# Two transformer blocks on one core: pool sums ahead of the rotary tiles, rotary partners shuffled on VectorE, and the FFN root applied to the up products

## What is computed

```python
def first_block(x, ...):
    h = rmsnorm(x, attn_norm[l])
    z = h @ w_in[l]                     # pool input, q, k, v, gates
    a = pool_mixer(u_pool, w_pool[l], pool_scale[l])     # windows 2, 4, 8, 16
    q = partial_rope(rmsnorm(q, q_norm[l]), positions) * scale
    k = partial_rope(rmsnorm(k, k_norm[l]), positions)
    b = swa_sink_attention(q, k, v, sinks[l])
    x = x + (g_pool * a + g_attn * b) @ w_out[l]
    h = rmsnorm(x, ffn_norm[l])
    up = causal_depthwise_conv(h @ w_up[l], conv_w[l], conv_b[l])
    gate, val = up[..., :D_FF], up[..., D_FF:]
    x = x + (jax.nn.silu(gate) * val) @ w_down[l]
...
def partial_rope(x, positions):         # first 16 of each head's 64 channels
    x1, x2, xp = xf[..., :half], xf[..., half:ROPE_DIM], xf[..., ROPE_DIM:]
    out = jnp.concatenate([x1 * cos - x2 * sin, x2 * cos + x1 * sin, xp], axis=-1)
...
def rmsnorm(x, g):
    r = lax.rsqrt(jnp.mean(xf * xf, axis=-1, keepdims=True) + EPS)
    return (xf * r * g.astype(jnp.float32)).astype(x.dtype)
```

## Time and profile before

| | us |
|---|---|
| median of 3 runs | 1557.7 (1555.8 to 1557.96) |
| the profiled execution: its time | 1557.63 |
| its span, first to last instruction | 1555.4 |
| PE busy in the span | 1422.1 (91%) |
| POOL busy | 782.1 (50%) |
| DVE busy | 666.7 (43%) |
| ACT busy | 420.2 (27%) |

### The profile page before, as it was taken

One profiled execution on the slowest core, in us unless ns is written; L12 is line 12 of the kernel. 1 busy time (PEld: TensorE's weight loads), 2 busy tenths in 40 slices (PEclk: granted clock), 3 DMA queues, 4 the chain that ended last, 5 costly groups with the idle time before them and its releaser, 6 DMA issues.

```text
span 1555.4 us, 20333 instructions
## 1 busy us (share of the span) xinstructions
PE 1422.1 (91%) x7602; PEld 1160.6 (75%) x7602; DVE 666.7 (43%) x1016; ACT 420.2 (27%) x833; POOL 782.1 (50%) x459
## 2 busy tenths in 40 slices
PE   5898789987999999999897999985997999999996
PEld 3776567766888888888796888755985888888884
DVE  5139455654534344211434888468625111211112
ACT  3132234431221112110323445452433111111111
POOL 4554234335566666666071633222362766666661
PEclk9999889998999999999998999996999999999998
DMA  4221121112232222222120111100020323322221
GB/s 171 82 81 68 35 74 55 67 40 97 76 100 95 94 94 94 96 98 90 43 96 27 41 58 53 56 0 2 2 78 31 121 95 99 101 97 94 94 81 54
DMA packets 31883, 114.00 MB, mean 73 GB/s; under 512 B 3536, under 2 KB 4048, under 8 KB 31568
## 3 DMA queue, kind: packets, MB, share of 16 engines
q1 hardware_dynamic: 31824, 113.16, 21.9%
HBM read 111.05 MB, written 2.10 MB: 73 GB/s over the span
## 4 chain that ended last, share of the span: by engine, by line
PE 81%; DVE 12%; ACT 3%; issue 2%; DMA 1%; POOL 0%; SPq 0%; DVEq 0%; ACTq 0%; POOLq 0%
PE ps L995 40%; PE ps L1189 17%; PE ps L1336 5%; ACT arena L542 3%; PE ps L1014 2%; PE ps L1035 2%; PE ps L1028 2%; PE ps L1209 1%; DVE arena L1948 1%; PE ps L1310 1%; PE ps L1140 1%; DVE arena L1613 1%; PE ps L1129 1%; DVE h_lo L1599 1%; DVE arena L1661 1%
## 5 line engine op out<-in xcount | busy, mean ns | idle before, releaser
L461 POOL TENSOR_SCALAR w_hi<-raw 128x1024 fp32r<-128x1024 f32 x204 | 220.0, 1078 | 650.8 <-PE ps L995 219.0
L463 POOL TENSOR_TENSOR w_lo<-raw,w_hi 128x1024 fp32r<-128x1024 f32 x204 | 512.2, 2511 | 17.1
L995 PE MATMUL ps<-h_hi,w_hi 128*128 128x512 f32 (+1 forms) x976 | 378.7, 394 | 12.9 <-ACT arena L542 7.4
L995 PE MATMUL ps<-h_lo,w_hi 128*128 128x512 f32 (+1 forms) x976 | 371.4, 386 | 0.0
L995 PE MATMUL ps<-h_hi,w_lo 128*128 128x512 f32 (+1 forms) x976 | 371.3, 386 | 0.0
L995 PEld LDWEIGHTS ps<-h_hi,w_hi 128*128 128x128 f32 x976 | 184.3, 191 | 58.7 <-issue 14.6
L995 PEld LDWEIGHTS ps<-h_lo,w_hi 128*128 128x128 f32 x976 | 184.0, 191 | 37.8 <-issue 2.5
L995 PEld LDWEIGHTS ps<-h_hi,w_lo 128*128 128x128 f32 x976 | 183.5, 190 | 36.5
L542 ACT ACTIVATE arena<-ps 128x512 f32<-128x512 f32 (+7 forms) x213 | 101.0, 509 | 308.0 <-PE ps L995 103.6
L542 ACT ACTIVATE arena<-arena 128x512 f32<-128x512 f32 (+6 forms) x190 | 101.0, 534 | 217.5 <-DVE arena L2193 134.2
L1189 PE MATMUL ps<-g_hi,w_hi 128*128 128x512 f32 x400 | 155.6, 389 | 0.0
(11 more groups left out here) (266 smaller groups left out, 1824.1 us busy)
## 6 DMA issues: line engine op xcount, KB each, us to landing
raw<-in_w_stream SPq DMA_DIRECT2D x204, 512.0 KB, 3.5
xT<-in_x_t SPq DMA_DIRECT2D x2, 1056.0 KB, 6.7
out<-xT SPq DMA_DIRECT2D x8, 256.0 KB, 2.1
C<-in_cst SPq DMA_DIRECT2D x1, 640.0 KB, 9.6
arena<-in_cst SPq DMA_DIRECT2D x1, 528.0 KB, 3.4
arena<-in_pos SPq DMA_DIRECT2D x1, 256.0 KB, 3.9
V<-in_vec SPq DMA_DIRECT2D x1, 174.5 KB, 8.1
band<-in_cst SPq DMA_DIRECT2D x1, 160.5 KB, 3.5
```

Source lines behind the costliest of these rows:

```text
L461: pool.tensor_scalar(w_hi[j][:], raw[j % 2][:], 1.0, 1.0, ALU.mult, ALU.mult).then_inc(S["pool_step"], 1)
L463: pool.tensor_tensor(w_lo[j][:], raw[j % 2][:], w_hi[j][:], ALU.subtract).then_inc(split_done[j], 1)
L995: last = mm(dst[p], w[:, k, :], h[:, k, cols], start=(k == 0 and n == 0), stop=(k == KT - 1 and n == 2))
```

## The change

Three parts.

1. **First rotary stage and pool sums.** `rot1` and the products by it go. DVE instead moves the partners with a `stream_shuffle` inside groups of 32 partitions (`ROT1`), and the sign goes into the sine table. `qk(t)` now starts when `qgb` is there and waits for the root only ahead of its last multiplication; `qk_side` no longer waits for `qk_dve`. On DVE all four `windows` and the first two `window_parts` stand ahead of `qk(0)`.
2. **Second rotary stage.** The same with `ROT2`: the products by `rot2` go, and two waits of `k2_side` with them.
3. **FFN.** The up products are made of x times gain without the root. ACT writes `h_hi` as x times gain as soon as the last `w_out` product is done, DVE subtracts (`low_of`); `sum_all(1)` stands behind the first pair of up tiles. DVE multiplies every one of the 44 up tiles by the root, in PSUM, before ACT reads it (`up_scaled`), and does so one tile ahead of the taps.

```diff
@@ -317,7 +304,7 @@
-            "up_act dve_up up_read silu_ready m1_ready relu_ready m2_ready ms_hi ms_ready f2_ready "
+            "up_scaled up_act dve_up up_read silu_ready m1_ready relu_ready m2_ready ms_hi ms_ready f2_ready "
@@ -397,6 +388,9 @@
+        ROT1 = [(m + 8 if m < 8 else m - 8) if m < 16 else m for m in range(32)]
+        ROT2 = [(m + 16) % 32 for m in range(32)]
...
@@ -667,11 +660,16 @@
-            for f in range(KT):
+            for f in range(KT - 1):
                 act.wait_ge(S["x_ready"], f + 1)
                 square(1, f, xT[:, f, REAL], T)
+            product(act, U_OUT + 7)
+            for f in range(KT):
+                if f == 2:
+                    act.wait_ge(S["x_ready"], KT)
+                    square(1, KT - 1, xT[:, KT - 1, REAL], T)
+                a(h_hi5[:, f, :], xT[:, f, REAL], ACT.Copy, scale=vcol("ffn_norm", f)).then_inc(S["hi_ready"], 1)
             root(1, ps[:, 7, :], first)
-            high(2, REAL)
...
@@ -1052,15 +1050,12 @@
             def qk_side(t):
                 pe.wait_ge(S["tile_read"], (9 if t == 0 else t + 10))
                 wait(pe, S["qk_sqrt"], t - 1)
-                wait(pe, S["qk_dve"], t - 1)
-                mm(ps[:, 2 + t % 2, :], cst_ap("blk64"), sqb[:, t % 2, :], start=True, stop=True)
-                mm(ps[:, 4 + t % 2, :], rot1, qgb[:, t % 2, :], start=True, stop=True).then_inc(S["qk_side"], 1)
+                mm(ps[:, 2 + t % 2, :], cst_ap("blk64"), sqb[:, t % 2, :], start=True, stop=True).then_inc(S["qk_side"], 1)
@@ -1159,13 +1154,12 @@
-            sum_all(1)
-
             def up(i):
                 for q in range(4):
                     if isinstance(i, int) and q < 2:
                         if q == 0:
                             tile_pair(U_UP, 2, [[ps[:, 0, :]], [ps[:, 1, :]]])
+                            sum_all(1)
                         continue
@@ -1235,14 +1229,10 @@
                 wait(pe, S["k2_sqrt"], t)
-                wait(pe, S["k2_dve"], t)
...
-                for c in range(2):
-                    last = mm(ps[:, 6 + c, 0:HALF], cst_ap("rot2"), val2[t % 2][:, halves[c]], start=True, stop=True)
@@ -1681,34 +1671,28 @@
             def qk(t):
                 out_ = KA if t == 0 else Q[:, t - 1, :]
-                dve.wait_ge(S["qk_sqrt"], t + 1)
+                dve.wait_ge(S["tile_read"], (9 if t == 0 else t + 10))
...
+                step(v.stream_shuffle(t2, qgb[:, t % 2, :], ROT1))
                 step(v.tensor_tensor(t1, qgb[:, t % 2, :], rope_c, ALU.mult))
-                step(v.tensor_tensor(t2, ps[:, 4 + t % 2, :], rope_s, ALU.mult))
+                step.settle()
+                step(v.tensor_tensor(t2, t2, rope_s, ALU.mult))
                 step.settle()
                 step(v.tensor_tensor(t1, t1, t2, ALU.add))
                 step.settle()
+                dve.wait_ge(S["qk_sqrt"], t + 1)
                 v.tensor_tensor(out_, t1, rs[:, t % 2, :], ALU.mult).then_inc(S["qk_dve"], 1)
...
+            for g in range(4):
+                windows(g)
+                if g < 2:
+                    window_parts(g)
+            for t in range(9):
+                qk(t)
             window_parts(2)
             window_parts(3)
...
+            def low_of(name, n, f):
+                dve.wait_ge(S["hi_ready"], parts_before(n) + f + 1)
+                v.scalar_tensor_tensor(out=h_lo5[:, f, :], in0=xT[:, f, REAL], scalar=vcol(name, f), in1=h_hi5[:, f, :],
+                                       op0=ALU.mult, op1=ALU.subtract).then_inc(S["h_ready"], 1)
...
-            add_squares(1, 7)
+            for f in range(KT):
+                low_of("ffn_norm", 2, f)
+                if f == 2:
+                    add_squares(1, 7)
             dve.wait_ge(S["rs_ready"], 2)
-            parts(2, REAL, gained("ffn_norm", REAL))
@@ -1815,6 +1806,12 @@
+                        if h == 0 and e == 0:
+                            product(dve, U_UP, i)
+                            v.tensor_tensor(ps[:, 0, :], ps[:, 0, :], n_ri[:, 0:T], ALU.mult).then_inc(S["up_scaled"], 1)
+                        if q < 3:
+                            product(dve, U_UP + q + 1, i)
+                            v.tensor_tensor(ps[:, q + 1, :], ps[:, q + 1, :], n_ri[:, 0:T], ALU.mult).then_inc(S["up_scaled"], 1)
                         dve.wait_ge(S["up_act"], 4 * i + q + 1)
```

More of the change, by code:

```diff
@@ L65 @@
     NV += _w
-_C = [("ident", P), ("blk64", P), ("rot2", P), ("swap", P), ("upto_f", P), ("upto_b", P),
+_C = [("ident", P), ("blk64", P), ("swap", P), ("upto_f", P), ("upto_b", P),
       ("past_f", P), ("past_b", P), ("neg_f", P), ("neg_b", P)]
@@ L74 @@
     NCST += _w
-NC1 = P + 256 + 64 + 1
+NC1 = 256 + 64 + 1
 NC2 = 2 * L
@@ L90, in constants @@
     put("swap", (i[:, None] == (i[None, :] + 64) % P).astype(np.float32))
-    rot2 = np.zeros((P, P), np.float32)
-    for m in range(P):
-        if m % 32 < 16:
-            rot2[m + 16, m] = -1.0
-        else:
-            rot2[m - 16, m] = 1.0
-    put("rot2", rot2)
     put("upto_f", (i[:, None] <= i[None, :]).astype(np.float32))
@@ L104, in constants @@
     c1 = np.zeros((P, NC1), np.float32)
-    for m in range(P):
-        if m % 64 < 8:
-            c1[m + 8, m] = -1.0
-        elif m % 64 < 16:
-            c1[m - 8, m] = 1.0
     k = np.arange(256)
     ok = (k[None, :] <= i[:, None] + P) & (i[:, None] + P - k[None, :] < P)
-    c1[:, P:P + 256] = np.where(ok, 0.0, -1e30)
+    c1[:, 0:256] = np.where(ok, 0.0, -1e30)
     for g, w in enumerate((2, 4, 8, 16)):
-        c1[:, P + 256 + 16 * g:P + 272 + 16 * g] = np.minimum(np.arange(16) + 1, w)
+        c1[:, 256 + 16 * g:272 + 16 * g] = np.minimum(np.arange(16) + 1, w)
     inv = np.float32(500000.0) ** (-np.arange(0, 16, 2, dtype=np.float32) / np.float32(16))
-    c1[:, NC1 - 1] = np.where(i % 64 < 16, inv[i % 8], 0.0)
+    c1[:, NC1 - 1] = np.where(i % 64 < 8, -inv[i % 8], np.where(i % 64 < 16, inv[i % 8], 0.0))
     t = np.arange(T)
@@ L681, in up @@
                         q = 2 * h + e
-                        product(act, U_UP + q, i)
+                        act.wait_ge(S["up_scaled"], 4 * i + q + 1)
                         if isinstance(i, int):
```

42 lines of the change are left out of this document (13 added, 29 removed).

## The result

The changed kernel takes 1539.2 us (median of 4 runs, 1536.5 to 1542.7) where the kernel before takes 1557.0 in the same session (4 runs, 1555.8 to 1558.0). The ratio is 0.9887 with a 95% interval of 0.9866 to 0.9909: 17.8 us faster. The forecast was 1536.3 with a range of 1526 to 1543.

The account below looks back on a forecast made before the run. The prediction took TensorE to bound the kernel (81% of the span, VectorE 12%). Gains of 12.7, 4.9 and 3.7 sum to 21.3 us: span 1534.1, time 1536.3, range 1526 to 1543.

Parts of the forecast that it names:

- Part 1: First rotary stage and pool sums: `pooled(0)` starts at 157.5 against 170.25, 12.7 us sooner.
- the period: First rotary stage, from query tile 2 on: a tile and one side product, 6.32 us, with DVE keeping up.
- the last step: End of the first rotary stage: `qk(7)`'s last multiplication at +4.7, then five instructions, `pooled(0)` 8.2 us behind query tile 8.
- Part 2: Second rotary stage: four side products fewer on the path, 3.55, and 2.1 at the end, less 0.7: 4.9 us faster.
- the later start of wide tile 2: Second rotary stage: DVE's shuffle and multiplications take turns with POOL's split, so wide tile 2 starts 0.7 us later (0 to 1.4).
- Part 3: FFN: 4.8 us gained at the third up tile, 1.1 waited at the down products: 3.7 us faster.
- The fourth: FFN: the pair of up tiles keeps its 12.46 us, clock included, since TensorE is still idle 4.6 us ahead of it.
- what follows is unchanged: Behind each mark on TensorE's list: later stages take the same time, so gains are not taken back.
- A: First rotary stage: pool sums hidden, no wait at the swap, part 1 gives 21 us, time 1528; chance 17%.
- B: First rotary stage: turns cost more, key tile 3 us later or periods add 4 to 6, time 1540 to 1543; 16%.
- C: The 44 up tiles: DVE's PSUM writes hold up TensorE, 0.69 us each, +30, time 1567; chance 4%.
- D: All three parts: gains taken back by waits behind them, time within 3 us of before; chance 3%.

Follow-up runs that it names:

- again: The changed kernel run once more with no edit, beside other kernels: 1540.6 us, ratio 0.9877 to the kernel before.
- sums_only: The kernel before with only the pool sums and their parts moved ahead of the key tile, rotary products left on TensorE: 1545.5 us, ratio 0.9923.
- part2_only: The kernel before with only the second attention's shuffles put in: 1552.9 us, ratio 0.9961.
- no_part3: The changed kernel with the up products' (FFN) part undone, the two rotary parts kept: 1543.0 us.
- part3_only: The kernel before with only the up products' (FFN) part put in: 1554.8 us, ratio 0.9973.
- old_order: The changed kernel with the sums over windows put back between the tiles, shuffles and all else kept: 1546.9 us, ratio 0.9938 to the kernel before.
- light_split: The changed kernel with GpSimd's second operation per weight tile replaced by one with a single tensor input, leaving out the weights' low halves: 1508.7 us, one run.
- scale_twice: The changed kernel with each up tile multiplied in PSUM twice, first by ones: 1538.6 us, ratio 0.9863 to the kernel before.
- best: The changed kernel with ScalarE's two Sin behind its fourth copy, and swap and transposes behind the first gate tile: 1527.1 us, ratio 0.9803.
- late_swap: The changed kernel with the key's swap and v's transposes moved behind the first gate tile: 1527.7 us, ratio 0.9802 to the kernel before.

## Why the prediction was right, and where its steps were off

The measured 1539.2 is 2.9 over the forecast of 1536.3, inside the range and inside the forecast's own 1532 to 1540; again, 1540.6, is just outside the latter. The mechanism was the one that was named. The gains by stretches of TensorE's timeline, against the kernel before (minus is faster):

| stretch | forecast | after | again |
|---|---|---|---|
| start to first tile | 0 | +2.1 | +0.3 |
| first tile to `pooled(0)` | -12.7 | -11.6 | -11.5 |
| `pooled(0)` to the last `w_out` product | 0 | +1.8 | +1.6 |
| last `w_out` product to the up pair | -5.7 | -5.7 | -5.7 |
| up pair to the squares | +2.0 | +3.0 | +3.2 |
| squares to step end | -4.9 | -6.0 | -6.1 |
| step end to next norm | 0 | -2.0 | +0.7 |
| next norm to the end | 0 | 0.0 | +1.0 |
| sum | -21.3 | -18.2 | -16.7 |

Mark by mark:

**Part 1, forecast -12.7, measured -9.5 and -11.3.** windows(3) was to end at 96.0 and the key tile at 102.3; again, which started as the kernel before did, has the shuffle behind windows(3) at 96.33 and the swap at 102.59. The wait at the swap was to be 5.9 and is 5.76, the period 6.32 and is 6.34, query tile 8 was to end at 149.4 and ended at 149.9. The shuffle priced at 0.70 by its neighbours took 0.72 to 0.75. Its place beside the split, by which the prediction fitted 3.5 and 3.5 us into 6.32, was another: none of the nine shuffles of the changed kernel ran beside a split, each came when the split was over, and the addition behind it ran into the next one (1.41 in place of 0.69). The period held with less to spare than was worked out: the shuffle and three more end 8.6 behind the tile's end and not 7.1, and VectorE's last idle times ahead of the root are 0.57, 0.48, 0.39 and 0.33 us, falling. That the period stayed TensorE's was close. What was off in the time is the last step: `pooled(0)` was to follow tile 8 by 8.2 us and followed by 9.1. The last multiplication of `qk(7)` was put at +4.7 from the tile's end; in the chain of the kernel after it ends at +5.4 (157.11 against 151.67), since the second multiplication and the addition ahead of it were both held by the split, and took 1.57 and 2.79 where their own length is 0.69:

```profile
151.41 0.58 DVE arena L1679
152.00 1.57 DVE arena L1681
153.60 2.79 DVE arena L1683
156.41 0.70 DVE arena L1686
```

Another 2.1 us of the first trace are the chance start. The prediction priced order and removed products as one sum; the runs show that the order carries four fifths of it.

**Part 2, forecast -4.9, measured -6.0.** Side products and the shorter end came as worked out: 4.30 of wait to 2.26 at the end is 2.04 where 2.1 was said. The term that was mis-sized is the later start of wide tile 2. It was charged 0.7 for the turns; from the squares to its start the time is 31.9 before, 32.0 after and 31.6 again, so next to nothing was lost. Without that charge the forecast would be 5.65, and from the start of wide tile 2 to the step end 6.0 were gained. And it is the old form that has no one price: 73.3 to 76.9 in four kernels, so the part is worth 2.4 to 6.0 by trace against trace, 4.2 against the old form's mean of 75.1. The forecast lies inside.

**Part 3, forecast -3.7, measured -2.65 by the first two traces.** Three of the four terms came as said: the pair starts 5.7 us sooner (4.64 behind the last `w_out` product, 4.6 was said), the wait at the end is 0.94 where 1.1 was said, and `sum_all` costs 0.86 where 0.87 was said. The fourth, that the pair keeps its 12.46, did not: by the chain it took 13.4 (374.15 to 387.56), 13.5 again. That is the term that was off, by 0.95 us of the 1.05, and it is off because the kernel before was lucky in the trace that I read: its pair ran 12.46 us, and the same old form ran 14.0 in sums_only (380.11 to 394.07), part2_only and no_part3. The old form waits twice ahead of the pair, 4.54 and 3.71 us, the new one once. From the pair's start to the squares before took 361.0, three kernels of the old form 362.5, the new form 364.0. Against these the part is worth 5.7 - 1.5 = 4.2; the medians say 3.7 (part3_only) and 2.4 to 3.8.

**What no term spoke of.** The start (2.1 against) and the delta rule's stage (2.0 for) are chance, since again shows +0.3 and +0.7 there, and they nearly cancel in the first trace. The first trace gained 3.1 us less than the forecast and again 4.6 less; that the median falls within 2.9 us is in part luck. The prediction's "what follows is unchanged" was wrong by 1.8 and 1.6: from `pooled(0)` to the last `w_out` product it is 206.95 us before, 208.7 after and 208.5 again. A part of it is the attention's first wait, 7.16 before, 8.47 after and 7.71 again (6.65 in old_order); what makes up the rest stays open. Such steps of one or two us would account for the 6 us between the fastest and the slowest execution of the changed kernel; that is argued, not shown.

**The rivals.** A (the sums are hidden) asked for no wait at the swap: there is one, and light_split shows what A would have needed, a lighter GpSimd. B (more contention) has its bounds at 1540 to 1543, and four of the changed kernel's eight executions fall there, but its mechanism, a key tile 3 us later or periods 0.5 to 1 us longer, did not occur; the 0.9 us of the last step are its only trace. C (VectorE's writes hold TensorE) is excluded by scale_twice. D (the gains are taken back) is excluded by the marks: 1.6 to 1.8 us were taken back, not 18.

**Still open.** Why TensorE's clock stays up behind some waits of 2 to 4 us and not behind others of the same length. That VectorE, with the turns it loses, is now the bound of the stage is argued from best and late_swap; a kernel with less VectorE work in it, or with some splits moved out of it, was not tried.

## What to carry to other kernels

Step through two engines that share a port turn by turn, with each instruction's own length; it gave a wait of 5.9 us where 5.8 came. Such turns hang on a microsecond: one instruction more and a split that began 1.1 us sooner made `qk(0)` 6.2 us long where it was 3.5. When work is moved ahead of a wait into an engine's "idle" time, look at once for the first consumer behind it: here moving that consumer (the swap) later was worth another 12 us, two thirds of what the whole change brought. And taking work off TensorE in a stage that VectorE paces gives back little: nine products of 0.86 were worth 2.

## What the runs showed of the hardware

- VectorE reading and writing PSUM in one instruction, 128x512 fp32 with one input in SBUF, takes 699 ns, as much as one that only reads PSUM there (681), and does not slow TensorE, which writes other banks meanwhile, even 88 times in a stage.
- `STREAM_SHUFFLE` of 128x512 fp32 took 0.72 to 0.76 us, with 0.01 for loading its mask, and as long beside GpSimd's split as without it: seven of the nine in late_swap and five in old_order lie on a running `w_hi` or `w_lo`, where the multiplication behind them waits.
- The level of TensorE's clock is not settled by the last wait alone: behind waits of 2.30 and 3.29 us the next matmuls ran at full clock (0.48 for the first), behind 3.15 in the kernel before the first took 0.78 and the granted clock was 0.73 in the 8 us from 782. In between lies sums_only: 0.48 for the first behind 3.55, then a granted clock of 0.76 from 775 to 782. The stretch from wide tile 2 to the step end scattered by 2.4 us between these four kernels, which do the same there.
- Turns are kept or lost in whole instructions: VectorE's angle step came out 2.0 us longer where GpSimd's `w_hi` began 0.2 us or more ahead of one VectorE instruction and not behind it, in kernels with the same code up to there. One SBUF input is no safeguard: of the angle step's `TENSOR_SCALAR` over 128x512, those ahead of GpSimd's start took 0.43, the two behind it 1.15 and 2.45.
